# Attention: which engine copies the turned probabilities out of the banks

## The reference

```
s = einsum(q, k) + bias          # masked or biased scores
p = softmax(s, axis=-1)          # some with a sink column
o = einsum(p, v)
```

## Time and profile before

| | us |
|---|---|
| median of three timed runs | 1814.29 |
| the profiled execution, its own time | 1817.45 |
| its span in the trace | 1816.2 |
| TensorE matmuls busy | 1777.4 (98%) |
| TensorE weight loads busy | 1656.5 (91%) |
| VectorE busy | 1352.7 (74%) |
| ScalarE busy | 1090.3 (60%) |
| GpSimd busy | 78.5 (4%) |

### The profile page before, as it was taken

The page is one execution under the profiler, slowest core; times in us unless marked ns, Lnnn a source line. Parts: engine busy times, 40 slices in busy tenths (PEclk is TensorE's granted clock), DMA queues, the critical chain, the costliest instruction groups (busy, mean ns, idle before and its releaser), DMA issues.

```text
span 1816.2 us, 37913 instructions
## 1 busy us (share of the span) xinstructions
PE 1777.4 (98%) x14762; PEld 1656.5 (91%) x14762; DVE 1352.7 (74%) x2948; ACT 1090.3 (60%) x2317; POOL 78.5 (4%) x81
## 2 busy tenths in 40 slices
PE   9999999999999999999999999999999999999997
PEld 7787999988989999999989998899999998689997
DVE  7676757578888876886687777886876888877766
ACT  5674646477666655665675656565664765565554
POOL 0001100020001000000020010100000000100000
PEclk9999999999999999999999999999999999999999
DMA  9959766886444645456555554456666543245663
GB/s 361 352 163 340 257 189 222 286 318 197 146 139 145 187 145 175 129 168 184 172 158 163 159 152 127 123 164 185 186 189 188 164 146 117 77 140 181 187 183 112
DMA packets 168610, 334.83 MB, mean 184 GB/s; under 512 B 19296, under 2 KB 21152, under 8 KB 168304
## 3 DMA queue, kind: packets, MB, share of 16 engines
q1 hardware_dynamic: 166752, 327.30, 56.6%
q0 software_dynamic: 1680, 5.11, 1.0%
HBM read 331.29 MB, written 1.05 MB: 183 GB/s over the span
## 4 chain that ended last, share of the span: by engine, by line
PE 92%; DVE 3%; DMA 2%; ACT 2%; issue 1%; SPq 1%; ACTq 0%; DVEq 0%
PE bank L620 25%; PE bank L621 24%; PE bank L622 24%; PE bank L1005 2%; PE bank L955 2%; PE bank L660 2%; PE bank L662 2%; PE bank L661 2%; PE bank L820 2%; PE bank L980 2%; PE bank L1312 1%; DMA ring_side<-in_stream 1%; DMA ring<-in_stream 1%; DVE Xx L1345 1%; PE bank L1990 1%
## 5 line engine op out<-in xcount | busy, mean ns | idle before, releaser
L594 DVE TENSOR_TENSOR low<-ring,high 128x512 fp32r<-128x512 f32 x820 | 556.2, 691 | 187.3 <-ACT high L586 176.6
L586 ACT CAST high<-ring 128x512 fp32r<-128x512 f32 x820 | 503.2, 619 | 311.5 <-PE bank L622 252.6
L620 PE MATMUL bank<-XHx,high 128*128 128x256 f32 x1720 | 502.2, 292 | 9.9 <-DVE XLx L1350 2.4
L621 PE MATMUL bank<-XLx,high 128*128 128x256 f32 x1720 | 485.6, 282 | 0.0
L622 PE MATMUL bank<-XHx,low 128*128 128x256 f32 x1720 | 484.9, 282 | 0.0
L620 PEld LDWEIGHTS bank<-XHx,high 128*128 128x128 f32 x1720 | 326.2, 190 | 31.7 <-issue 12.8
L621 PEld LDWEIGHTS bank<-XLx,high 128*128 128x128 f32 x1720 | 326.9, 190 | 0.9
L622 PEld LDWEIGHTS bank<-XHx,low 128*128 128x128 f32 x1720 | 326.7, 190 | 0.0
L586 ACT CAST high_side<-ring_side 128x512 fp32r<-128x512 f32 x220 | 135.2, 618 | 78.8 <-DMA ring_side<-in_stream 73.8
L594 DVE TENSOR_TENSOR low_side<-ring_side,high_side 128x512 fp32r<-128x512 f32 x220 | 152.5, 702 | 37.5 <-ACT high_side L586 32.6
L620 PE MATMUL bank<-XHc,high_side 128*128 128x256 f32 x608 | 176.6, 291 | 3.0 <-DVE low_side L594 3.0
(11 more groups left out here) (471 smaller groups left out, 3590.7 us busy)
## 6 DMA issues: line engine op xcount, KB each, us to landing
ring<-in_stream SPq DMA_DIRECT2D x820, 256.0 KB, 3.0
ring_side<-in_stream SPq DMA_DIRECT2D x220, 256.0 KB, 2.9
ring_mod<-in_stream SPq DMA_DIRECT2D x96, 512.0 KB, 7.7
x_nb<-in_rpb POOLq DMA_DIRECT2D x6, 256.0 KB, 3.6
x_late_NB<-in_rpb POOLq DMA_DIRECT2D x6, 256.0 KB, 3.2
Xx<-in_x SPq DMA_DIRECT2D x2, 512.0 KB, 5.8
Xc<-in_ctx SPq DMA_DIRECT2D x1, 1024.0 KB, 5.9
out<-y SPq DMA_DIRECT2D x8, 128.0 KB, 2.0
```

The costliest lines, as they stand in the source:

```text
L586: nc.scalar.copy(st.high[:, j % st.n_split, :], st.ring[:, j % st.n_ring, :]).then_inc(*A.tick(st.s_high, A_us(st.tb * P), (st.name, "high ...
L594: nc.vector.tensor_tensor(st.low[:, j % st.n_ring, :], st.ring[:, j % st.n_ring, :], st.high[:, j % st.n_split, :].bitcast(F32), ALU.subtr ...
L620: nc.tensor.matmul(out, wh, xh, start=(i == 0), stop=False)
L621: nc.tensor.matmul(out, wh, xl, start=False, stop=False)
```

## The change

The function that decides which engine does a copy now always says ScalarE. VectorE's call of `turned_copies` issues nothing any more.

```diff
 def copies_on_scalar(i, pair):
-    return (pair + i + 1) % 2 == 0
+    return True
```

## The result

The changed kernel takes 1820.0 us (median of six runs, 1819.02 to 1823.09) against 1815.9 us before, measured beside it (six runs): a ratio of 1.003, interval 1.0019 to 1.0041, so about 5 us slower. The forecast was 1812.5 us, faster by 1.8, with a range up to 1819.5. It was wrong in direction, and the median lies just outside the range. The kernel before itself measured 1.6 us higher here than the 1814.29 us on which the forecast was built; that shift isn't the change's. The same kernel measured again in a later set (e3) gave 1.0027, interval 1.0016 to 1.0037.

What follows compares the result with a forecast made beforehand. TensorE was taken as the bound, busy 1777.4 of 1816.2 us. The terms -0.5 - 0.4 - 0.6 - 0.5 + 0.2, with the order at 0, made -1.8, so 1814.29 became 1812.5 us, range 1806.5 to 1819.5.

Steps and rivals of the forecast that it cites:

- (f): Whole run: the planner's changed clocks reorder instructions from the first attention on; taken as 0, bounds -2.5 and +2.5 us.
- (a): Last attention, stall at 1553.6: without its copy VectorE delivers the low parts earlier; 0.5 us saved, bounds 0 and 2.0.
- (b): Last attention, low clock behind two halts of TensorE: recovers in proportion as they shorten; 0.4 us saved, bounds 0 and 2.4.
- (c): Last attention: VectorE's normalisations that TensorE waits for move up without the copy ahead; 0.6 us saved, bounds 0 and 0.9.
- (d): Odd attention, 440 to 560: TensorE's waits for VectorE shrink; 0.5 us saved, bounds 0 and 1.7.
- (e): Attentions: ScalarE's longer queue delays casts and copies that TensorE needs; 0.2 us lost, bounds 0 and 4.6.
- Rival 3: The new order makes a stall elsewhere, a late low part: +2.5 us, +2.4 more with the clock, 1816.8 to 1819.2; chance 0.23.
- Rival 2: Layer 1's attention: ScalarE becomes the late engine as eight copies join its chain, +4.6 us, 1818.9; chance 0.10.
- Rival 1: Layer 1's attention: VectorE's relief dissolves the stalls and the low clock, -6.6 us or -8.3 with the odd attention, 1807; chance 0.22.

Runs made afterwards that it cites:

- e3: The changed kernel, unedited, measured again beside the kernel before: 1.0027 of before.
- e2: The changed kernel with its planned order kept, but half of the copies still issued to VectorE by the old rule: 1.0043 of before.
- e1: The kernel before with its order kept and VectorE still charged by the planner, but every copy issued to ScalarE: 0.9985 of before.
- e5: The changed kernel with TensorE's context recurrence planned only after the last odd head's values: 1.0020 of before.
- e11: The changed kernel with the planner's assumed duration of each turned copy 0.05 us longer: 1.0012 of before.
- e12: The changed kernel with the planner's assumed duration of each turned copy 0.05 us shorter: 1.0063 of before.
- e14: e12 with TensorE's context recurrence planned only after the last odd head's values: 1.0039 of before.
- e15: The changed kernel with the layer 1 embedding's ScalarE and VectorE parts ranked earlier by the planner (2 to -2): 1.0035 of before.
- e9: The kernel before with its order kept, only the last attention's twelve VectorE copies issued to ScalarE: 0.9986 of before.
- e10: The kernel before with its order kept, but all 100 copies issued to VectorE: 1.0020 of before.
- e13: The kernel before with copies on ScalarE alone only in the odd attention, replanned from there: 1.0066 of before.
- e6: The kernel before with copies on ScalarE alone in all attentions but the odd one, replanned: 1.0002 of before.
- e7: The kernel before with the planner's assumed duration of each turned copy 0.05 us longer, engines unchanged: 1.0027 of before.

## Why the prediction was wrong

- **The step that failed is (f), the planner's order.** It was costed at nothing, with a single stall more or less, 2.5 us, as its bounds. Measured in two pairs, e2 against before and e3 against e1, it is +0.43 and +0.42%, 7.8 us, most of it TensorE waiting longer (46.7 and 48.0 us of idle time against 38.8 and 38.2). It was noticed, and treated as a lottery with mean zero. That was the error: as far as these runs go, the order of before is no draw from the middle. Six kernels have all copies on ScalarE and a replanned order (the changed one, e5, e11, e12, e14, e15), and they lie between 1.0012 and 1.0063. The seventh has before's order and is at 0.9985. Neither nudge of the kernel before was free either. The bound was also too narrow because it was taken from one stall, where a new order changes the list from the first attention on.
- **(a), the stall at 1553.6: right.** 0.5 us forecast, 2.0 to 1.5 us in e1, by the mechanism described, and it stayed bounded by the scores. In the changed kernel this wait vanished altogether, through the order.
- **(b), the clock: under-sized, its mechanism open.** 0.4 us forecast, bounds 0 and 2.4. The timed executions of e1 and e9 have mean clocks 0.0009 and 0.0012 above before's, an estimated 1.7 and 2.2 us of gains of 2.7 and 2.5. The forecast tied the clock to the length of the two halts, and they hardly shrank (3.3 to 2.8 us) while the clock of the stretch went from 0.96 to 1.00. No run shows what lifted it, and e10, with longer halts, has 1.00 there as well (below).
- **(c), the normalisations: right in kind, under-sized.** 0.9 us of waits, 0.6 forecast to go; in e1 and e9 all went.
- **(d), the odd attention: about right in size, not in kind.** 0.5 us forecast. In e1 the stretch from 440 to 560 is idle for 1.6 us, 2.0 before and in e9. But TensorE still waits 0.9 us for L1078 there, 0.8 before; what went is one of the two waits for low parts. 0.4 us can't be told apart in the times of e1 and e9.
- **(e), ScalarE's queue: right.** 0.2 us forecast; at a fixed order TensorE's one wait for ScalarE in the last attention stayed at 1.3 us. The wait for L1198 of 2.5 us in the changed kernel is there in e2 too, in the kernel's whole list of waits, with half of the copies on VectorE, so it is the order's.
- **The sum of (a) to (e)** was -1.8 us; the move at a fixed order is worth -2.7 (-4.4 to -1.1). So the sum was sound in size, with too little for the clock and for (c).
- **The rivals.** Rival 3 named what happened, a stall made elsewhere by the new order, with its sign, and its 1816.8 to 1819.2 is near the outcome; it was given 0.23, of which 0.09 counted as no change. It expected one late low part; the longest new waits are for the recurrence's input and for ScalarE's embedding copies, there are several, and the order costs 7.8 us in all, not 2.5 to 4.9. Rival 2 is refuted as the cause here: at a fixed order all copies on ScalarE are faster (e1), and all on VectorE slower (e10). Rival 1 didn't come about: in e1 the halts at L660 and L1005 still stand, 1.5 and 1.3 us.

The Trainium skill gives its rule of using both ScalarE and VectorE for evacuation ("TensorEngine Tiling (Array Packing)", section PSUM Bottleneck) for a TensorE sped up by tiling, where the copy may become the bottleneck. Here TensorE holds 92% of the chain and the copies are no bottleneck; ScalarE alone was the faster (0.9985), so the measurement decides against using both in this kernel.

What stays open is which of the many places of the new order carry the rest of its cost. The recurrence's place is a likely one, by e13 against e6 and by e12 against e14, whose intervals overlap a little. The wait for the embedding is not a handle. Why e6 and e13 don't add up is unexplained, and so is why before's order is better than its neighbours.

**The version to keep** is e1, or e9, which is the same within the intervals: 1812.2 and 1811.9 us, 0.9985 and 0.9986 of before, faster than both kernels. The copies go to ScalarE, and the planner goes on believing that they don't.

## What to carry to other kernels

Where a planner writes the order out of assumed durations, an edit is two edits: the work that moves, and a new order for everything behind it. Measure them apart, by issuing the new work at the old order and the old work at the new one. Before costing the second at zero, nudge an assumed duration by a few hundredths of a microsecond and see what an order is worth: here 0.3%, twice what the edit itself could bring, and in both directions of the nudge a loss. And a long wait in the trace is a place, not yet a cause: 6.1 us of waits for one line could be taken away and bring nothing. Where the list of matmuls is the same, compare TensorE's idle time and its granted clock before crediting a gain to shorter waits.

## What the runs showed of the hardware

The granted clock in one stretch differs between executions of one kernel, with the same idle time. The stretch from 1530 to 1610 of the changed kernel's first profile is shown above (76.89 us busy, clock 1.00). The same stretch in e3, the same kernel:

```profile
1530.00:1610.00 80.00, 76.89 (x559) 62.40 (x558) 58.29 (x149) 52.52 (x125) 8.81 (x8) 0.98 0.32 99
```

and in e10, which is idle for longest there:

```profile
1530.00:1610.00 80.00, 74.07 (x539) 59.66 (x539) 71.03 (x170) 41.64 (x101) 8.46 (x8) 1.00 0.30 92
```

The same 3.1 us of idle time go with 1.00 once and 0.98 once, and 5.9 us with 1.00, where 4.2 us had 0.96 before. In e7 and e13 TensorE's three longest waits in this stretch are those of the kernel before (2.0, 1.3 and 0.7 us), and the first line, e7's, has 1.00 and the second, e13's, 0.96:

```profile
1530.00:1610.00 80.00, 75.86 (x555) 61.44 (x554) 65.58 (x157) 46.45 (x111) 8.50 (x8) 1.00 0.32 97
...
1530.00:1610.00 80.00, 75.89 (x533) 60.02 (x532) 62.91 (x151) 44.58 (x105) 8.05 (x8) 0.96 0.30 91
```

So a clock price read from one profiled execution, as in (b), is that execution's, and no more than a possible one for the kernel. The mean over many timed executions says more: for the kernel before it lies between 0.9927 and 0.9929 in five sets of 12 to 29.
